# Convolved feed-forwards by Strassen's scheme from the seventh tile on

## The reference

```
def conv_glu_ffn(xn, w_up, conv_w, conv_b, w_down):
    u, gt = split_cols(xn @ w_up, (D_FF, D_FF))     # D_FF = 2752
    u = causal_dwconv(u, conv_w, conv_b)            # 3 taps along the tokens, one set per column
    return (jax.nn.silu(u) * gt) @ w_down
```

## Time and profile before

| | us |
|---|---|
| median of 3 runs | 3077.11 (3075.03 to 3077.15) |
| profiled execution, its own time | 3075.32 |
| profiled execution, span in the trace | 3073.5 |
| TensorE busy | 2989.0 |
| VectorE busy | 1740.0 |
| ScalarE busy | 1273.2 |
| GpSimd busy | 318.3 |

### The profile page before, as it was taken

The page is one execution under the profiler, slowest core; times in us unless marked ns, Lnnn a source line. Parts: engine busy times, 40 slices in busy tenths (PEclk is TensorE's granted clock), DMA queues, the critical chain, the costliest instruction groups (busy, mean ns, idle before and its releaser), DMA issues.

```text
span 3073.5 us, 41491 instructions
## 1 busy us (share of the span) xinstructions
PE 2989.0 (97%) x17696; PEld 2463.2 (80%) x17696; DVE 1740.0 (57%) x2154; ACT 1273.2 (41%) x1702; POOL 318.3 (10%) x285
## 2 busy tenths in 40 slices
PE   8999989999999999999999998999999999999999
PEld 6877778778887767778887775789998888878998
DVE  6445464556544766456544755666666553566665
ACT  5443443443322564443323545544444333344442
POOL 1010001010000001010000200133310000013340
PEclk9999999999999999999999999999999999999999
DMA  5341123233332311233332330233333222223331
GB/s 188 110 117 29 43 79 122 96 83 96 96 89 93 104 55 63 89 83 96 96 93 89 94 89 14 66 100 97 103 103 107 86 86 86 81 77 103 105 105 66
DMA packets 340104, 274.89 MB, mean 89 GB/s; under 512 B 28768, under 2 KB 308832, under 8 KB 339408
## 3 DMA queue, kind: packets, MB, share of 16 engines
q1 hardware_dynamic: 335552, 252.83, 27.5%
q0 software_dynamic: 4368, 19.41, 1.8%
HBM read 263.83 MB, written 8.39 MB: 89 GB/s over the span
## 4 chain that ended last, share of the span: by engine, by line
PE 87%; DVE 6%; ACT 5%; issue 2%; POOL 0%; DMA 0%; DVEq 0%; SPq 0%; ACTq 0%; POOLq 0%
PE ps L190 86%; ACT arena L204 2%; ACT whi L207 1%; DVE arena L213 1%; DVE arena L221 1%; DVE wlo L213 1%; PE ps L193 1%; DVE hT L213 1%; ACT L204 0%; DVE xlo L221 0%; POOL arena L213 0%; DVE sml L230 0%; ACT arena L207 0%; DVE split L213 0%; ACT split L207 0%
## 5 line engine op out<-in xcount | busy, mean ns | idle before, releaser
L190 PE MATMUL ps<-split,whi 128*128 128x512 f32 (+1 forms) x3008 | 886.7, 373 | 16.3 <-DVE hT L213 7.7
L213 DVE TENSOR_TENSOR wlo<-wraw,whi 128x2048 fp32r<-128x2048 f32 (+5 forms) x261 | 565.9, 2171 | 485.8 <-ACT whi L207 485.5
L190 PE MATMUL ps<-xhi,whi 128*128 128x512 f32 (+2 forms) x2040 | 764.5, 380 | 18.5 <-DVE xlo L213 7.1
L190 PE MATMUL ps<-xhi,wlo 128*128 128x512 f32 (+2 forms) x1984 | 742.0, 374 | 0.0
L190 PE MATMUL ps<-xlo,whi 128*128 128x512 f32 (+2 forms) x1944 | 730.5, 376 | 0.0
L190 PEld LDWEIGHTS ps<-split,whi 128*128 128x128 f32 x3008 | 548.3, 188 | 133.4 <-issue 24.6
L207 ACT ACTIVATE whi<-wraw 128x2048 fp32r<-128x2048 f32 (+5 forms) x261 | 457.0, 1754 | 337.8 <-PE ps L190 237.4
L190 PE MATMUL ps<-split,wlo 128*128 128x512 f32 (+1 forms) x1504 | 553.2, 368 | 0.0
L190 PEld LDWEIGHTS ps<-xhi,whi 128*128 128x128 f32 (+1 forms) x2040 | 381.1, 189 | 103.7 <-issue 15.7
L190 PEld LDWEIGHTS ps<-xhi,wlo 128*128 128x128 f32 (+1 forms) x1984 | 374.2, 189 | 68.9 <-issue 4.5
L190 PEld LDWEIGHTS ps<-xlo,whi 128*128 128x128 f32 (+1 forms) x1944 | 366.3, 188 | 68.4
(11 more groups left out here) (132 smaller groups left out, 2431.4 us busy)
## 6 DMA issues: line engine op xcount, KB each, us to landing
wraw<-in_ffn_w_up SPq DMA_DIRECT2D x128, 512.0 KB, 5.1
wraw<-in_odd_w_in SPq DMA_DIRECT2D x24, 1024.0 KB, 5.1
wraw<-in_ffn_w_gate SPq DMA_DIRECT2D x44, 512.0 KB, 3.9
wraw<-in_ffn_w_down SPq DMA_DIRECT2D x20, 1024.0 KB, 5.1
wraw<-in_ffn_w_down SPq DMA_DIRECT2D x24, 768.0 KB, 4.4
wraw<-in_xattn_wkv SPq DMA_DIRECT2D x16, 1024.0 KB, 5.6
wraw<-in_xattn_wq SPq DMA_DIRECT2D x8, 1024.0 KB, 5.2
wraw<-in_xattn_wo SPq DMA_DIRECT2D x8, 1024.0 KB, 5.2
```

The source lines that it names most:

```text
L190: return self.e.matmul(out, lhsT, rhs, start=start, stop=stop, skip_group_check=True)
L213: return self.e.tensor_tensor(out, a, b, op)
```

## The change

`ffn` is written anew, after the pattern of `folded`. Tiles 0 to 5 are computed as before, tiles 6 to 21 by the seven products, with the convolution on the u half of the result. Tiles are taken in another order: the last three of the matrix (19, 20 and the half tile 21) come first, so that the half tile is third. Only tiles 0 and 1 alternate u and g. Groups are of three tiles, the down projection of a group has two units of 512 columns. On the side of the input, the sums t1 to t4 and their low parts are made by GpSimd, the high parts by ScalarE after tiles 1, 2 and 3. The sums s1, s2, s4 of even tiles lie in one buffer, those of odd tiles in the second quarter of `X8` that no Strassen product reads (B12), in three pieces. In a Strassen tile VectorE gates and finishes the tile before between its additions. The weights of the first down projection's second unit are made before tile 5's chain.

The core of the diff (`...` where lines are left out; the old `ffn`, 175 lines, goes; `norm` becomes `FreshKept`, which keeps the normalised input in float32; `product` and `quarters` are those of `folded`):

```diff
@@ -357,10 +357,12 @@
 for raw, hi, _ in first:
     act.copy(hi, raw)
 if n in self.folded:
-    sums, hi, _, maker, tile = self.folded[n]
+    parts, maker, tile = self.folded[n]
     act.wait_ge(maker.of("sums", tile))
     act.copy(final[1], final[0]).then_inc(*self.made_hi.up("quarters", n))
-    act.copy(hi, sums).then_inc(*self.made_hi.up(n))
+    for sums, hi, _ in parts[:-1]:
+        act.copy(hi, sums)
+    act.copy(parts[-1][1], parts[-1][0]).then_inc(*self.made_hi.up(n))
 else:
     act.copy(final[1], final[0]).then_inc(*self.made_hi.up(n))
 self.n_hi += 1
@@ -375,8 +377,11 @@
     dve.tt(lo, raw, hi.bitcast(F32), ALU.subtract)
 if n in self.folded:
     dve.tt(final[2], final[0], final[1].bitcast(F32), ALU.subtract)
-    sums, hi, lo, _, _ = self.folded[n]
+    parts = self.folded[n][0]
     dve.wait_ge(self.made_hi.of(n))
+    for sums, hi, lo in parts[:-1]:
+        dve.tt(lo, sums, hi.bitcast(F32), ALU.subtract)
+    sums, hi, lo = parts[-1]
     dve.tt(lo, sums, hi.bitcast(F32), ALU.subtract).then_inc(*self.made_lo.up(n))
 else:
     dve.tt(final[2], final[0], final[1].bitcast(F32), ALU.subtract).then_inc(*self.made_lo.up(n))
...
+def ffn(stage, l, w_u, w_g, w_down, ends, prev, nxt):
+    S = Stage(stage, sem)
+    S.carry = carry = nxt(S)
+    nt, H, FIRST, HALF = 22, 256, 6, 2
+    tile_of = [19, 20, 21] + list(range(19))
+    size = [64 if n == HALF else P for n in range(nt)]
+    at[0] = 0
+    hid = [als() for _ in range(6)]
+    tb, gb = [al(T), al(T)], [al(T), al(T)]
+    half = gb[1]
+    x_at = at[0]
+    al(3 * 2 * 1024)
+    s_at = at[0]
+    al(4 * 1536)
...
+    if at[0] > NORM_AT:
+        raise ValueError(f"arena {at[0]}")
+    kept = arena[:, s_at:s_at + 4096].rearrange("p (k n) -> p k n", k=8)
...
+    def sums_of(n):
+        if n % 2 == 0:
+            return tuple(sums[:, i * T:(i + 1) * T].rearrange("p (k n) -> p k n", k=4) for i in range(3))
+        return free12[0][:, :, 0:P], free12[0][:, :, P:H], free12[1][:, :, 0:P]
+    def group_of(n):
+        return min(n // 3, 6)
...
+    downs = []
+    for i, g in enumerate(groups):
+        r = tile_of[g[0]] * P
+        w = w_down[r:r + sum(size[k] for k in g), :]
+        downs.append([((f"down{i}", "unit", b0), [(w[:, b0:b0 + 512], 0)], 512,
+                       [((f"down{i}", b0 // P + m), m) for m in range(4)]) for b0 in (0, 512)])
...
+    def extra(q):
+        return tuple(split[:, s_at + (2 * q + i) * 1536:s_at + (2 * q + i + 1) * 1536] for i in range(2))
+    def fold(n):
+        m = W.number[W.stage, ("up", n)]
+        hi, lo = extra(m % NSPL)
+        if n % 2 == 0:
+            parts = [(sums, hi, lo)]
+        else:
+            parts = [(src, *(t[:, i * T:i * T + T].rearrange("p (k n) -> p k n", k=4) for t in (hi, lo)))
+                     for i, src in enumerate(sums_of(n))]
+        W.folded[m] = (parts, S.G, n)
+        return m
+    def place(n):
+        return hid[n % 6] if n < 21 else Src(split[:, x_at:x_at + T], split[:, x_at + T:x_at + 2 * T])
...
+        def seven(n):
+            u = W.take(("up", n), *unit(n))
+            e = extra(fold(n) % NSPL)
+            a, b, c, d = (ps.take(name, n) for name in "abcd")
+            pe.wait_ge(W.ready(("up", n)), ps.empty("a", n), norm.made(7))
+            product(a, u, e, "a11", "b11", True, "p1", n)
+            pe.wait_ge(ps.empty("b", n))
+            product(b, u, e, "a12", "b21", True, "p2", n)
+            pe.wait_ge(ps.empty("c", n), S.G.of("t1"))
+            product(c, u, e, "s1", "t1", True, "p5", n)
+            pe.wait_ge(ps.empty("d", n), S.G.of("t4"))
+            product(d, u, e, "a22", "t4", True, "p4", n)
+            pe.wait_ge(S.A.of("p1", n), S.G.of("t2"))
+            product(a, u, e, "s2", "t2", False, "u2", n)
+            pe.wait_ge(S.A.of("p5", n))
+            product(c, u, e, "s4", "b22", False, "c12", n)
+            pe.wait_ge(S.A.of("u2", n), S.G.of("t3"))
+            product(a, u, e, "s3", "t3", False, "u3", n, unit=("up", n))
...
+                i_.then_inc(*up(S.P, "u", n, unit=("up", n)))
+                return
+            both = [(("u", n), 0), (("g", n), P)]
+            for cols in [both] if n < 2 else [both[0:1], both[1:2]]:
+                bs = [ps.take(*key) for key, _ in cols]
...
+        def convolved(n):
+            m, t, y, c = size[n], tile_of[n], tb[n % 2][0:size[n], :], cb[n % 2]
+            w = [par_col("ffn_conv_w", (l, j), t)[0:m, :] for j in range(3)]
+            dve.wait_ge(S.A.of("u", n) if 1 < n < FIRST else NEVER, S.V.own())
+            dve.ts(y, c[0:m, 0:T], w[0], par_col("ffn_conv_b", l, t)[0:m, :], ALU.mult, ALU.add).then_inc(*up(S.V))
+            for j in (1, 2):
+                dve.wait_ge(S.V.own())
+                dve.stt(y, c[0:m, j:j + T], w[j], y, ALU.mult, ALU.add).then_inc(*up(S.V, "conv", n, j))
+        def gated(n):
+            y = tb[n % 2][0:size[n], :]
+            if n >= FIRST:
+                dve.wait_ge(S.A.of("silu", n), S.V.own())
+                dve.tt(y, y, gb[n % 2], ALU.mult).then_inc(*up(S.V, "hid", n))
+            elif n == HALF:
+                dve.wait_ge(S.A.of("silu", n), S.A.of("half"), S.V.own())
+                dve.tt(y, y, half[0:64, :], ALU.mult).then_inc(*up(S.V, "hid", n))
+            else:
+                dve.wait_ge(S.A.of("silu", n), S.P.of("g", n), S.V.own())
+                dve.tt(y, y, ps.ap("g", n), ALU.mult).then_inc(*up(S.V, "hid", n, frees=("g", n)))
+        def finish(n):
+            d = place(n)
+            dve.wait_ge(S.A.of("hid_hi", n), S.V.own())
+            dve.tt(d.lo[0:size[n], :], tb[n % 2][0:size[n], :], d.hi[0:size[n], :].bitcast(F32),
+                   ALU.subtract).then_inc(*up(S.V, "hid_lo", n))
...
+        def added(n, bank):
+            c, g = cb[n % 2], gb[n % 2]
+            dst, made, was = {"b": (c[:, 2:H + 2], "p2", "p1"), "c": (c[:, H + 2:T + 2], "c12", "u2"),
+                              "d": (g[:, 0:H], "p4", "u3"), "a": (g[:, H:T], "u3", "p5")}[bank]
+            dve.wait_ge(S.P.of(made, n), S.A.of(was, n))
+            dve.tt(dst, dst, ps.ap(bank, n)[:, 0:H], ALU.add).then_inc(*up(S.V, bank, n, frees=(bank, n)))
+        def up_tile(n):
+            W.rest(dve, ("up", n) if n != FIRST - 1 else downs[0][0][0])
+            if n >= FIRST:
+                added(n, "b")
+                if n > FIRST:
+                    gated(n - 1)
+                    finish(n - 1)
+                added(n, "c")
+                convolved(n)
+                added(n, "d")
+                added(n, "a")
+                return
+            if n < 2:
+                dve.wait_ge(S.P.of("u", n), norm.root())
+                dve.tt(cb[n % 2][:, 2:T + 2], ps.ap("u", n), norm.rs, ALU.mult).then_inc(*up(S.V, frees=("u", n)))
+            convolved(n)
+            if n < 2:
+                y = tb[n % 2]
+                dve.wait_ge(S.A.of("silu", n), norm.root())
...
+        for what, n in order():
+            if what == "up":
+                up_tile(n)
+            else:
+                if n == 5:
+                    gated(21)
+                    finish(21)
+                for name, _, _, blocks in downs[n]:
+                    W.rest(dve, name if n else downs[0][1][0])
+                    for key, m in blocks:
+                        d = h(key[-1])
+                        dve.wait_ge(S.P.of(*key), S.V.own())
+                        dve.tt(d, d, ps.ap(*key), ALU.add).then_inc(*up(S.V, "h", *key, frees=key))
+                        if n == 6 and key[-1]:
+                            carry.vector(dve, key[-1] - 1)
+                if n == 6:
+                    carry.vector(dve, 7)
...
+        def high(name):
+            x, hi, lo = tq[name]
+            act.wait_ge(S.G.of(name, "sum"))
+            act.copy(hi, x).then_inc(*up(S.A, name))
...
+        def kept_(n, name):
+            c, g = cb[n % 2], gb[n % 2]
+            bank, dst = {"p1": ("a", c[:, 2:H + 2]), "p5": ("c", g[:, H:T]), "u2": ("a", c[:, H + 2:T + 2]),
+                         "u3": ("a", g[:, 0:H])}[name]
+            act.wait_ge(S.P.of(name, n), S.V.of("conv", n - 2, 2), S.V.of("hid", n - 2) if n >= FIRST + 2 else NEVER)
+            act.copy(dst, ps.ap(bank, n)[:, 0:H]).then_inc(*up(S.A, name, n))
+        def up_tile(n):
+            W.round(act, ("up", n) if n != FIRST - 1 else downs[0][0][0])
+            if n >= FIRST:
+                kept_(n, "p1")
+                if n > FIRST:
+                    silu(n - 1)
+                kept_(n, "p5")
+                if n > FIRST:
+                    finish(n - 1)
+                kept_(n, "u2")
+                kept_(n, "u3")
+                return
+            if n > 1:
+                c, m = cb[n % 2], size[n]
+                act.wait_ge(S.P.of("u", n), S.V.of("zeroed"), S.V.of("conv", n - 2, 2))
+                if n == HALF:
+                    act.copy(half[0:64, :], ps.ap("u", n)[64:P, :]).then_inc(*up(S.A, "half"))
```

(62 more changed lines are left out.)

257 lines of the change are left out of this document (102 added, 155 removed).

## The result

The changed kernel takes 3102.15 us (median; 3100.52 to 3103.32, 4 runs) beside 3077.13 for the kernel before on the same chip: 1.0087 times as long, 95% interval 1.0075 to 1.0099, slower by 25 us. The forecast was 3096, the range 3055 to 3114.

A forecast was written before the change was run, and what follows sets the result against it. TensorE, busy 97% of the span, was taken as the bound, with VectorE slow at the start. Per stage -13.85 + 18.1 + 4.3 + 1.7 = +10.3, two stages +20.5 on 3075.3 us: forecast 3096, range 3055 to 3114.

The forecast's parts named there:

- the start: Each stage's first tiles to tile 6: VectorE meets GpSimd's operations and makes TensorE wait, 18.1 us a stage.
- the steady part: Later Strassen tiles: TensorE waits for ScalarE's copy of bank a where a group begins, 4.3 us a stage.
- the clock: TensorE's granted clock falls after the 10 us wait: 1.7 us lost a stage, 0 to 3.4.
- TensorE's columns: Sixteen Strassen tiles a stage, each 0.80 us shorter on TensorE than a full tile: -12.8 us a stage.
- the old waits: TensorE's two waits for weights' low halves in each convolved feed-forward, 0.85 and 0.20 us, would go.
- unit 1 of the first down projection: Second unit of the first down projection: TensorE waits 10.1 us for its weights' low half from VectorE.
- unit 7: Weights behind the chains of tiles 3 and 4 in VectorE's queue: ready at 738.2, wanted at 728.2, 10.1 late.
- The handover: Second stage's end, handing over two sums of squares: GpSimd gets 2.6 us a block; allowed 1.5 us either way.
- -13.85: TensorE's saving a stage if VectorE were never late: shorter tiles, -12.8, and the two old waits gone.
- 1: Rival at the shared port: GpSimd waits, not VectorE, so it costs nothing on the path; 3054 us, chance 0.24.
- 2: Rival at the shared port: it costs half, the start 10 us instead of 18; 3079 us, chance 0.14.
- 3: Rival in the steady tiles: VectorE falls behind, 1.5 us in each of 11 later tiles; 3125 us, chance 0.07.

The follow-up runs named there:

- e11: e7 with the high and low halves of the input's sums made beside tiles 6 and 7 instead of tiles 1 to 3; 3057.4 us, ratio 0.9944.
- e3: Changed kernel with ScalarE keeping bank a after the sixth product before making the high half of the tile before; 3092.4 us, ratio 1.0060.
- e4: Changed kernel with VectorE instead of GpSimd adding the second sum of squares at the second stage's handover; 3100.4 us, ratio 1.0089.
- e9: Kernel before with eight unused GpSimd subtractions of 1024 elements added to each convolved feed-forward's start; 3100.8 us, ratio 1.0087.
- e6: e5 with the scheme starting at the ninth tile instead of the seventh; 3084.5 us, ratio 1.0030.
- e2: Changed kernel with the input's 8 wide operations (sums and low halves) on VectorE instead of GpSimd; 3102.4 us, ratio 1.0095.
- e10: e7 with the input's sums and low halves made by GpSimd again; 3066.1 us, ratio 0.9970.
- e1: Changed kernel without GpSimd's input sums and low halves; ScalarE copies plain quarters of the input in their place; 3087.5 us, ratio 1.0045.
- e5: Changed kernel with VectorE doing the previous tile's gating and low half between a tile's steps in the first six tiles; 3098.0 us, ratio 1.0073.
- e7: Changed kernel with the edits of e2 to e5 at once and the scheme from the ninth tile on; 3060.1 us, ratio 0.9956.

## Why the prediction was right, and which terms were off

The mechanism and the sign were right: GpSimd's work makes VectorE late, and TensorE waits for it. That the total of a stage fits, +10.1 for +10.3, is luck in part: the start was walked 4.0 too high, the steady part 1.9 and the clock 1.6 too low.

- **TensorE's columns, -12.8.** Not to be read alone in the changed kernel. e11's first stage is the nearest: 14 Strassen tiles (-11.2), the old waits gone (-1.05), new ones of 1.0 and no clock give -11.3; measured -10.2.
- **The start, +18.1, measured 14.1.** Tile 3 3.09 (3.2); unit 1 of the first down projection 10.08 (10.1); tile 6 0.95 (3.8); unit 0 none (1.0). The walk had unit 7 ready at 738.2 and tile 6's bank at 750.1; they came at 740.9 and 753.3, so VectorE was 3 us later than walked; tensor_scalar, counted as free, is the likely reason (below). The 10.1 fits because two misses cancel: unit 7 came 2.7 us later, and TensorE was ready for it at 730.8 instead of 728.2. TensorE lost 1.7 to the clock behind tile 3's wait and 1.7 to the half tile, less the 1.0 that it didn't wait for unit 0. In unit 0 a block of nine matmuls takes 2.47 us, not 9 x 0.2267 = 2.04, since around its three matmuls of 64 rows the starts lie 0.32 to 0.33 us apart. The kernel before pays the same in its last group, so this moved into the start and adds nothing to the stage. Tile 6 waited less because TensorE itself was late: unit 1 took 11.5 us for 8.2, again 1.7 of clock and 1.7 of the half tile.
- **The clock, +1.7, measured 3.3 and 3.5.** Both waits cost 1.7, not one.
- **The steady part, +4.3, measured 4.43 as idle time** but 6.2 as time of the stage, by e3, which also shows that the order on ScalarE was its cause.
- **The handover, 1.5 either way, measured about +7.** This is the term that was mis-sized: 5.1 of wait and 1.8 of clock. "GpSimd gets 2.6 us of work a block" was set against blocks of 2.72 us as if it met nobody there. In the rows below it begins its last six additions only at 1724.45, behind VectorE's low half of the next stage's weights (2.63 us, at 1719.25) and the addition to `hT` that waits behind it. The six take 9.25 us, 1.54 each instead of 1.29, since they meet VectorE, the very rule that the start was walked with. Before, the same low half stood there (GpSimd's four additions took 7.67 then and 7.29 now), but with blocks of 4.08 us only two additions were left behind it. By e4 GpSimd's share was 3.3 of the 5.1.
- **The sum.** The terms of the first stage as measured, -13.85 + 14.1 + 4.4 + 3.3, give +8.0. With 6.2 for the steady part they give +9.8; 0.3 of its +10.1 stay, of which 0.25 is a wait of TensorE for ScalarE's square at the stage's end. The range's upper end, 3114, doesn't follow from its own terms: 3109 and 1.5 make 3110.5.
- **The Trainium skill** (SBUF — State Buffer, section SBUF: two separate sides) says that VectorE takes the shared port also for an operation in a 2-port mode, not only for one with two SBUF inputs. The trace agrees in so far as tensor_scalar, one SBUF input, waits for GpSimd; the mode itself is in no row. It took 1.85, 1.69, 2.60, 2.22 and 1.49 us beside GpSimd in the first stage, 0.54 without it. By that rule the forecast would have been 3105, 3 above the measured time where mine is 6 below; but mine misses by the handover, not by the stage. On VectorE these five cost 7.1 us, the four ahead of unit 7's end 6.2. That is more than the 2.7 us by which unit 7 came later than walked: the walk had charged part of the same GpSimd time to the scalar_tensor_tensor behind.
- **Rivals.** 1 fell by e9. 2 (half the price) isn't refuted by the start, 14.1, which lies between its 10 and my 18; it fell by VectorE's rows, where the meetings up to 740 cost 18 us for the 16 that I had walked, and by GpSimd's 2.4 to 2.5 us an operation. 3 fell: no wait for weights in the steady part, in either stage.

GpSimd at the handover, after, with VectorE's row between; then GpSimd before:
```profile
1715.74 7.29 POOL L213 TENSOR_TENSOR arena<-arena 128x512 f32<-128x512 f32 x4 [1.36 <-ACT arena L204]
...
1719.25 2.63 DVE L213 TENSOR_TENSOR wlo<-wraw,whi 128x2048 fp32r<-128x2048 f32 x1 [4.05 <-ACT whi L207]
...
1724.45 9.25 POOL L213 TENSOR_TENSOR arena<-arena 128x512 f32<-128x512 f32 x6 [1.42 <-ACT arena L204]
```
```profile
1696.10 7.67 POOL L213 TENSOR_TENSOR arena<-arena 128x512 f32<-128x512 f32 x4 [2.85 <-ACT arena L204]
1705.19 2.96 POOL L213 TENSOR_TENSOR arena<-arena 128x512 f32<-128x512 f32 x2 [1.42 <-ACT arena L204]
```

## What to carry to other kernels

Work given to an idle GpSimd isn't free where VectorE has no slack: in e9 each meeting cost VectorE 2.0 us for a GpSimd instruction of 2.4, so put such work where VectorE is slack (e6, the clearest gain), or on VectorE, which gained nothing in e2 and little in e10. Walk the end of a stage with the same rule as its start. And after an edit compare stages by a fixed instruction at their heads, with the clock beside: a wait removed can come back as slow columns.

## What the runs showed of the hardware that was not expected

- VectorE's tensor_scalar with one SBUF input stands behind GpSimd's instruction like the operations with two (2.60 for 0.54 us).
- The clock's price is not read off the wait's length. Behind 10.08 us it lost 1.7, behind 6.49 (e1) 6.1, behind 4.17 (e5) 6.2, behind 2.19 in e7 nothing in the first stage and 5.1 in the second. What decides it stays open; nothing here was run for it.
- A block of nine matmuls with three of 64 rows among them takes TensorE 2.47 us instead of 2.04 (after, 723.31 to 725.79), with no wait in it, in the kernel before as well.
- Identical work ahead of the first stage lost between 3.3 and 10.1 us to the clock from one profiled run to the next.
